# Expert layers of a one-core flow-matching step: rows by indirect DMA through DRAM instead of placement matmuls

## What is computed

```python
g_i = top1(softmax(x @ w_rg + b_rg))               # one of 4 groups
e_i, e_v = top2(logits of the 8 experts in it)     # two experts of the group
gate = softmax(e_v) * g_p
combine[n, e] = sum over the two choices of one_hot(expert) * gate
hid = silu(x @ w_g[e]) * (x @ w_u[e])              # 1024 -> 256 for every expert e
y = sum over e of (combine[:, e] * hid) @ w_d[e]   # 256 -> 1024
x = x + m[5] * y                                   # gated residual
```

## Time and profile before

| | us |
|---|---|
| median of three runs | 1170.89 |
| profiled execution, first to last instruction (span) | 1167.8 |
| of it: expert loop of layer 0, first gate-up product to last down product | 324.6 to 610.3 |
| of it: expert loop of layer 1 | 847.6 to 1133.3 |
| TensorE busy | 1052.6 (90% of the span) |
| DVE busy | 543.4 (47%) |
| ACT busy | 277.1 (24%) |
| GpSimd busy | 58.8 (5%) |

### The profile page before, as it was taken

How to read it: one execution, slowest core, us unless ns; L and a number is a source line. 1 busy time by engine, 2 the same in 40 slices (tenths; PEclk the granted TensorE clock), 3 DMA queues, 4 the chain that set the end, 5 groups by cost and what they waited for, 6 DMA issues and landing times.

```text
span 1167.8 us, 12636 instructions
## 1 busy us (share of the span) xinstructions
PE 1052.6 (90%) x4586; PEld 547.0 (47%) x4586; DVE 543.4 (47%) x1082; ACT 277.1 (24%) x526; POOL 58.8 (5%) x80
## 2 busy tenths in 40 slices
PE   2899999698899999999997998898599999999981
PEld 0254455454445545545443465444444545545540
DVE  0224256724524544555447264614525545544545
ACT  0312222302222222222223114302122222222221
POOL 3010000200200000000001000010200000000000
PEclk9799999899899999999997998998799999999995
DMA  9981622544789999898898623021969889889701
GB/s 296 390 288 71 219 71 76 188 176 179 294 334 358 353 356 358 331 368 341 331 366 316 198 73 118 1 77 66 402 264 370 344 330 368 342 355 356 290 18 54
DMA packets 69991, 294.43 MB, mean 252 GB/s; under 512 B 5888, under 2 KB 5952, under 8 KB 44488
## 3 DMA queue, kind: packets, MB, share of 16 engines
q1 hardware_dynamic: 66296, 278.58, 62.8%
q0 software_dynamic: 3664, 15.43, 3.8%
HBM read 291.81 MB, written 2.18 MB: 252 GB/s over the span
## 4 chain that ended last, share of the span: by engine, by line
PE 84%; DVE 7%; ACT 4%; SPq 2%; DMA 1%; issue 1%; DVEq 0%; POOL 0%; ACTq 0%
PE psum L893 19%; PE psum L621 19%; PE psum L915 10%; PE psum L851 5%; PE psum L852 4%; PE psum L881 4%; PE psum L882 4%; PE psum L860 3%; PE psum L651 2%; PE psum L709 2%; PE psum L743 2%; PE psum L868 1%; PE psum L610 1%; PE psum L820 1%; SPq L412 1%; DMA x<-in_x_sample 1%
## 5 line engine op out<-in xcount | busy, mean ns | idle before, releaser
L621 PE MATMUL psum<-ring,ht 128*128 128x512 f32 (+1 forms) x576 | 233.4, 563 | 0.7 <-ACT ht L1035 0.7
L893 PE MATMUL psum<-ring,arena 128*64 128x512 f32 x1024 | 226.8, 595 | 1.6 <-ACT arena L1202 1.6
L621 PEld LDWEIGHTS psum<-ring,ht 128*128 128x128 f32 x576 | 109.1, 192 | 116.8 <-issue 111.8
L893 PEld LDWEIGHTS psum<-ring,arena 128*64 128x64 f32 x1024 | 71.5, 137 | 134.1 <-issue 134.1
L1618 DVE TENSOR_TENSOR ht<-ht,psum 128x512 f32<-128x512 f32 x192 | 118.4, 683 | 4.2 <-PE psum L882 3.4
L915 PE MATMUL psum<-ring,arena 128*64 128x512 f32 x512 | 116.9, 598 | 0.0
L851 PE MATMUL psum<-h_top,places 128*128 128x512 f32 x204 | 85.6, 420 | 4.4 <-DVE places L1599 4.4
L881 PE MATMUL psum<-y_top,slots_t 128*128 128x512 f32 x192 | 81.1, 422 | 8.1 <-DVE y_low L1627 8.1
L852 PE MATMUL psum<-h_low,places 128*128 128x512 f32 x204 | 82.0, 402 | 0.0
L882 PE MATMUL psum<-y_low,slots_t 128*128 128x512 f32 x192 | 78.2, 407 | 0.0
L1623 DVE TENSOR_SCALAR slots_t<-arena 128x384 fp32r<-128x384 f32 x32 | 11.5, 360 | 138.6 <-ACT arena L1209 138.6
(11 more groups left out here) (270 smaller groups left out, 1087.1 us busy)
## 6 DMA issues: line engine op xcount, KB each, us to landing
ring<-in_w_exp_gate SPq DMA_DIRECT2D x32, 2048.0 KB, 7.4
ring<-in_w_exp_up SPq DMA_DIRECT2D x32, 2048.0 KB, 11.9
ring<-in_w_exp_down SPq DMA_DIRECT2D x32, 2048.0 KB, 8.1
ring<-in_w_mod SPq DMA_DIRECT2D x24, 2048.0 KB, 13.7
ring<-in_w_in_even SPq DMA_DIRECT2D x5, 2048.0 KB, 20.2
shift_scale<-mod_rows POOLq DMA_DIRECT2D x3, 2048.0 KB, 11.1
ring<-in_w_in_odd SPq DMA_DIRECT2D x3, 2048.0 KB, 15.9
ring<-in_w_out_even SPq DMA_DIRECT2D x2, 2048.0 KB, 9.1
```

The costliest lines, as they stand in the source:

```text
L621: mm = pe.matmul(psum[:, to, 0:cols], HT[:, k, b * P:(b + 1) * P], w[:, k, :], start=(k == 0), stop=(k == KC - 1))
L893: mm = pe.matmul(psum[64 * e:64 * e + 64, 2, :], XT[:, k, 64 * e:64 * e + 64], RG[:, 3 * v:3 * v + 2, e, k, :], start=(k == 0), stop=(k == ...
```

## The change

Rows are no longer moved by matmuls. ACT stores `h` to a DRAM tensor `h_rows`. Once a layer DVE and TensorE make a table with a column for each pair: for each of the 128 slots the token's row, the row of the result tensor, and the gate. For each pair GpSimd looks up a column, fetches the rows of `h` by an indirect DMA (a pair ahead, into one of two buffers `XS`), and sends the gated result from one of two buffers `Y` to the DRAM tensor `y_rows` by another. `y_rows` has a row for each entry (token, choice), 768 in all. Empty slots carry a row number that is out of bounds (4095, or 3711 for a fetch), which `bounds_check` is there to leave out. After the loop ACT loads `y_rows` back in six loads of 512 KB, two for each block, and DVE adds the two choices, multiplies and adds to `x`. The rounded copies, the `places` matrices and the matmuls L851/L852, L881/L882 and L868 go away, as does the 128x3072 memset of the sum. In layer 0 the load of the next shift and scale rows (2 MB) moves from after the expert loop to before it, on GpSimd's queue. The diff, cut:

```diff
+PLACES = MAX_ROUNDS * PAIRS + 4
+NOWHERE = 4096.0
...
 # GpSimd
             def experts(l):
                 u = 2 * l + 1
                 store_rest(f"norm_{u}")
-                pool.wait_ge(S("turned"), 6 * (TURNS.index(u) + 1))
-                pool.wait_ge(S("h_top"), l + 1)
-                pool.tensor_tensor(H_LO, H, H_HI, ALU.subtract).then_inc(S("h_split"), 1)
                 if l == 0:
                     store_rest("router")
                     store_rest("places")
                 pool.wait_ge(S("x_updated"), NB * u)
                 load_rows(u, (2, 3), gt_t[:, :], "gate_in")
+                if l == 0:
+                    pool.wait_ge(S("h_ready"), NB * (u + 1))
+                    load_rows(2, (0, 2), gs_t[:, :], "rows_in")
...
+                def gather(q, v, static=False):
+                    pool.tensor_copy(one(from_row[v][:, 0:1].bitcast(U32)), column(0, q, static)).then_inc(M("row_looked_up"), 1)
+                    pool.wait_ge(M("row_looked_up"), q + 1)
+                    pool.sem_inc(S("pool_waited"), 1)
+                    pool.indirect_dma_start(XS[v], None, h_rows[l], bass.IndirectOffsetOnAxis(ap=from_row[v][:, 0:1].bitcast(U32), axis=0),
+                                            bounds_check=T - 1, oob_is_err=False).then_inc(M(f"gathered_{v}"), 16)
+
+                def pair(q, v, static=False):
+                    pool.wait_ge(M("x_ps"), q * 2 + 2)
+                    pool.sem_inc(S("pool_waited"), 1)
+                    gather(q + 2, v, static)
+                    if not static:
+                        pool.wait_ge(M(f"scattered_{v}"), (q - v) * 8)
+                        pool.sem_inc(S("pool_waited"), 1)
+                    pool.tensor_copy(one(to_row[v][:, 0:1].bitcast(U32)), column(1, q, static)).then_inc(M("place_looked_up"), 1)
+                    pool.tensor_copy(one(to_row[v][:, 1:2]), column(2, q, static)).then_inc(M("place_looked_up"), 1)
+                    pool.wait_ge(M("place_looked_up"), q * 2 + 2)
+                    pool.wait_ge(M("y_sb"), q * 2 + 2)
+                    pool.sem_inc(S("pool_waited"), 1)
+                    pool.indirect_dma_start(y_rows[l], bass.IndirectOffsetOnAxis(ap=to_row[v][:, 0:1].bitcast(U32), axis=0), Y[v], None,
+                                            bounds_check=2 * T - 1, oob_is_err=False).then_inc(M(f"scattered_{v}"), 16)
...
 # TensorE
+                pe.wait_ge(S("entries_ready"), l + 1)
+                for i in range(6):
+                    mm = pe.matmul(psum[:, 6, 0:2 * PLACES], in_slot[:, i, :], in_pair[:, i], start=(i == 0), stop=(i == 5))
+                mm.then_inc(S("table_ps"), 1)
                 if l == 0:
                     mod_products(mods("places")[0])
                     mod_sum(mods("places")[0])
...
+                def turn_rows(q, v, first=False):
+                    pe.wait_ge(M(f"gathered_{v}"), 16 if first else (q - v) * 8 + 16)
                     for half in range(2):
...
                     mm.then_inc(M("gate_up"), 1)
-                    gather(q + 1, 1 - v)
+                    turn_rows(q + 1, 1 - v, first)
                     pe.wait_ge(M("hidden"), q + 1)
...
-                    if not first:
-                        combine(q - 1)
-                    turn_rows(q + 1)
                     pe.wait_ge(M("hidden_t"), q + 1)
...
-                    weights_back(q, v, first)
...
 # ACT
+                act.wait_ge(S("h_ready"), NB * (u + 1))
+                act.dma_start(h_rows[l].rearrange("(b p) n -> p b n", p=P), H).then_inc(S("h_stored"), 16)
...
-                    rows_copies(q + 1)
                     x_copies(q + 1)
-                    weights_copy(q, first)
-                    act.wait_ge(M("weights_sb"), q + 1)
+                    act.wait_ge(M("place_looked_up"), q * 2 + 2)
+                    if not first and not second:
+                        act.wait_ge(M(f"scattered_{v}"), (q - v) * 8)
...
+                for v in range(2):
+                    act.wait_ge(M(f"scattered_{v}"), R * 128)
+                for b in range(NB):
+                    for j in range(2):
+                        act.dma_start(YS[j][:, b, :], y_rows[l][(NB * j + b) * P:(NB * j + b + 1) * P]).then_inc(M(f"y_back_{b}"), 16)
...
 # DVE
-                link(dve.memset(ht_t[:, :], 0.0))
...
+                dve.scalar_tensor_tensor(slot_c, i_a, float(PAIRS), ef, ALU.mult, ALU.add)
+                link(dve.scalar_tensor_tensor(slot_p, i_a, float(-HALF), p6, ALU.mult, ALU.add))
+                link(dve.scalar_tensor_tensor(slot_p, odd, float(HALF), slot_p, ALU.mult, ALU.add))
+                dve.tensor_tensor(in_slot, across(P), along(slot_p, P), ALU.is_equal)
+                link(dve.tensor_tensor(in_pair[:, :, 0, :], across(PLACES), along(slot_c, PLACES), ALU.is_equal))
+                link(dve.tensor_tensor(in_pair[:, :, 1, :], in_pair[:, :, 0, :], along(gates.rearrange("p j b -> p (j b)"), PLACES), ALU.mult))
+                dve.tensor_tensor(in_pair[:, :, 0, :], in_pair[:, :, 0, :], along(dest, PLACES), ALU.mult).then_inc(S("entries_ready"), 1)
...
+                dve.wait_ge(S("table_ps"), l + 1)
+                found = psum[:, 6, 0:PLACES]
+                dve.tensor_copy(tab[:, 2, :], psum[:, 6, PLACES:2 * PLACES])
+                link(dve.tensor_scalar(tab_tmp, found, 0.0, NOWHERE, ALU.is_equal, ALU.mult))
+                link(dve.scalar_tensor_tensor(tab[:, 1, :], found, -1.0, tab_tmp, ALU.add, ALU.add))
+                link(dve.tensor_scalar(tab_tmp, tab[:, 1, :], float(T), float(-T), ALU.is_ge, ALU.mult))
+                dve.tensor_tensor(tab[:, 0, :], tab[:, 1, :], tab_tmp, ALU.add).then_inc(S("table_ready"), 1)
...
                 for b in range(NB):
-                    link(dve.tensor_tensor(UPD_M[b % 2], ACC[:, b, :], GT[:, min(b, 1), :], ALU.mult))
-                    dve.tensor_tensor(X[:, b, :], X[:, b, :], UPD_M[b % 2], ALU.add).then_inc(S("x_updated"), 1)
+                    dve.wait_ge(M(f"y_back_{b}"), 32)
+                    link(dve.tensor_tensor(YS[0][:, b, :], YS[0][:, b, :], YS[1][:, b, :], ALU.add))
+                    link(dve.tensor_tensor(YS[0][:, b, :], YS[0][:, b, :], GT[:, min(b, 1), :], ALU.mult))
+                    dve.tensor_tensor(X[:, b, :], X[:, b, :], YS[0][:, b, :], ALU.add).then_inc(S("x_updated"), 1)
```

184 lines of the change are left out of this document (57 added, 127 removed).

## The result

The changed kernel took 1140.55 us (median of four runs, 1140.17 to 1143.99) beside 1170.26 us (1169.29 to 1171.95): 0.9744 of the time before, with a 95% interval of 0.9726 to 0.9762. The profiled execution's span went from 1167.8 us to 1138.8, 29.0 us less, where the prediction's sum had 32.7.

A forecast was written before the change was run, and what follows sets the result against it. TensorE was taken to bound both expert loops, the weight stream close behind. Loops -84.2, heads +7 and +29.5, tails +4 and +11 sum to -32.7 us: 1170.9 - 32.7 = 1138 us, range 1092 to 1186 us.

The forecast's parts named there:

- The pair: Both expert loops: weights (14.9 to 16.0 us) plus rows (0.9 to 1.0) set a pair's period, taken as 16.2 us.
- the 423 GB/s of the stretch with nothing to wait for: Stretch 815 to 845 us: six weight transfers at a full DMA share, which makes a pair's weights 14.9 us.
- the 393 scaled from the loop before: Expert loops: 350 GB/s at 0.89 DMA share scaled to 393 at 1.0, making a pair's weights 16.0 us.
- TensorE's 13.2 us: TensorE's need per pair after the change: 7.0 gate-up, 2.5 hidden values' wait, 3.65 down products.
- the hidden values' chain: Each pair, gate-up products' end to down products' start: ACT, DVE, two transposes, DVE and hand-overs, about 2.5 us.
- The loops: End of first gate-up to end of last down products: 278.6 to 236.5 us, gain 42.1 per layer, 84.2 in both.
- the 9.7 us allowed for them: A loop's start and end beside 14 x 16.2: 1.5 issue and landing, less 5, plus 13.2 of TensorE.
- The heads: Before first gate-up products: layer 0 loses 29.5 us (fetch held behind loads on its queue), layer 1 loses 7.
- The tails: Last down products to last addition to `x`: 21.5 us in layer 1 (loss 4), 29.7 in layer 0 (loss 11).
- that rival: Clock falls in each pair's weight wait, slowing half the next gate-up products: 14 us more, 1152 us; chance 0.11.
- Empty slots: Rival: indirect DMAs move all 128 rows, some 18.0 us a pair, 50 us more, 1188 us; chance 0.12.
- GpSimd: Rival: GpSimd's indirect DMAs bind; at 10 us each, 22 us a pair, some 160 us more, 1300 us; chance 0.14.

The follow-up runs named there:

- the fetch-first runs: GpSimd's first two fetches put ahead of what stands in front on its queue, or only of the 2 MB load, against the changed kernel: 1125.18 and 1134.08 us.

## Why the prediction was right

The forecast was 1138 us, and 1140.55 came. The mechanism held: the weight stream with the rows in it sets the pair, and part of the gain goes in heads and tails. That the sum came so close is partly luck, since its terms are off by up to 7 us and cancel. Step by step:

**The pair.** Its 16.2 us were 15.95 by bytes. The run with a quarter of the down weights shows that the weight stream sets it; of the two parts, weights 14.9 to 16.0 and rows 0.9 to 1.0, the run without rows gives 15.06 and 0.88. Of the two rates in the working, the 423 GB/s of the stretch with nothing to wait for was near the loop's 418, and the 393 scaled from the loop before was not. TensorE's 13.2 us were 12.7 when nothing else held it: the hidden values' chain, put at 2.5 us, takes 2.1 from the gate-up products' end to the down products' start (461.8 to 463.84). The Trainium skill's rule (page "DMA: Bandwidth & Descriptors", section "Where 436 GB/s comes from"), that the HBM side binds at about 358 GB/s, is not what the loops show: 417 to 418 GB/s over 220 and 210 us, on one core, and the run without rows has its weights alone at that rate.

**The loops** went from 278.6 to 237.5 and 240.0 us where 236.5 was worked out. The pairs were shorter than 16.2, by 3.5 us in 14, and the start and end longer than the 9.7 us allowed for them: 237.5 - 14 x 15.95 = 14.2, and 16.7 in layer 1. Part of that is the fallen clock. The last two pairs of layer 0:

```profile
566.64 9.84 PE L908 MATMUL psum<-ring,arena 128*64 128x512 f32 x32 [3.36 <-DMA ring<-in_w_exp_up]
...
582.56 7.09 PE L908 MATMUL psum<-ring,arena 128*64 128x512 f32 x32 [0.21 <-issue]
```

The last wait for weights of a loop is ahead of the last pair but one. Its gate-up products take 9.84 us (9.97 in layer 1) at the fallen clock (0.54 granted from 565 to 570 us), and the last pair waits for nothing, so these 2.7 us have no later wait to vanish in. No run tests this alone: in the run with unused matmuls such matmuls stand ahead of the last pairs too. What the rest of the 4.5 and 7.0 us is stays open.

**The heads.** Layer 0 lost 26.2 us against 29.5: the first gate-up products ended at 357.9 instead of 361, since gate rows' load and fetch started some 3 us earlier than worked out. The cause was the right one, as the fetch-first runs show. Layer 1 lost 9.4 us, counted from the norm's last step, against 7: the table took 4.37 us for 4.2, but the rows were there 6.5 us after GpSimd's issue ended (841.25 to 847.79) instead of 2, with weights still loading beside the fetch (420 GB/s from 840 to 845 us). The landing was mis-sized by 4.5 us and the head by only 2.4, because a gain had been put at nothing: the change also takes the rounding of `h`, the memset and GpSimd's subtraction out of DVE's way, and from the norm's last step to the slot steps it is 21.5 us in layer 1 instead of 24.4.

**The tails** grew to 29.6 and 22.1 us, against 29.7 and 21.5. (The sum took a loss of 11 us for layer 0, where its own 29.7 less 18.0 is 11.7; 11.6 came.)

**The rivals.** The clock does alternate as that rival had it: after most of the longer waits (3.0 to 4.6 us) the gate-up products take 8.5 to 10 us, after most of the shorter ones (up to 2.1 us) 7.1. The Trainium skill, page "TensorE: Matmul & The Clock Gate", section "HAM oscillation", describes such a pattern of DMA wait and slow step, and the trace agrees with it (granted clock 0.94 in the loops), except that here about every second step is slow and not every one. What falls is its price: with the full clock through the whole loop the time was the same. Empty slots don't move rows. GpSimd needs two issues of 1.03 us a pair, and a third cost only what its packets did.

## What to carry to other kernels

Taking work from the engine that is full gains only down to the next limit, and that limit is found by adding the bytes of a stage at the rate that a stretch with nothing to wait for shows (here 423 GB/s against the loop's 418). A fetch that a stage's start needs belongs ahead of every transfer on its queue that is needed later, and ahead of the wait for what those transfers send. Where two streams are close, look for what is given back at the ends: of 80 us gained in the loops, 52 were lost in heads and tails, and 22 of these came back, by the medians, with another order on one queue and TensorE kept at work in the heads. Work that a change takes away in passing, such as a copy or a memset ahead of a stage, belongs in the sum as well.
